# A decoder layer in split fp32 on one core: four of eight GLU chunks as seven block products, and the convolution steps handed out anew

## What is computed

```
xn = RMSNorm(x)
proj = xn @ w_in                     # B_a C_a X_a | V_b G_b | Q | three gates
ya = (a_b * dwconv3(a_c * a_x)) @ w_out_a
ub = b_val * sigmoid(b_glu)          # the GLU: G_b and V_b, 1024 columns each
yb = dwconv31(ub)                    # causal, per channel, 31 taps
yb = silu(layernorm(yb + bias)) @ w_out_b
yx = softmax(Q K^T / 16) V @ w_out_x # cross attention, 4 heads
merged = g0 * ya + g1 * yb + g2 * yx ; h = x + merged @ w_o
h = h + (silu(hn @ w_ff_gate) * (hn @ w_ff_up)) @ w_ff_down ; final RMSNorm
```

## Time and profile before

| | |
|---|---|
| median of 3 runs | 1070.38 us (1069.89 to 1071.01) |
| the profiled execution's own time | 1069.33 us |
| its span, first to last instruction | 1067.6 us |
| TensorE busy | 1057.3 us, 99% |
| VectorE busy | 718.2 us, 67% |
| ScalarE busy | 479.7 us, 45% |
| GpSimd busy | 110.8 us, 10% |
| mean granted TensorE clock | 0.997 of full |
| DMA | 187.25 MB, mean 175 GB/s |

### The profile page before, as it was taken

How to read it: one execution, slowest core, us unless ns; L and a number is a source line. 1 busy time by engine, 2 the same in 40 slices (tenths; PEclk the granted TensorE clock), 3 DMA queues, 4 the chain that set the end, 5 groups by cost and what they waited for, 6 DMA issues and landing times.

```text
span 1067.6 us, 20526 instructions
## 1 busy us (share of the span) xinstructions
PE 1057.3 (99%) x8751; PEld 1051.1 (98%) x8751; DVE 718.2 (67%) x1234; ACT 479.7 (45%) x550; POOL 110.8 (10%) x93
## 2 busy tenths in 40 slices
PE   9999999999999999999999999999999999999997
PEld 9999999999999999999999999999999999999996
DVE  6766677888888654686323755578778457588754
ACT  6744443453335353344345723344456245366431
POOL 3661000002300000000000000000000000000000
PEclk9999999999999999999999999999999999999998
DMA  8967886689796878758876663231578365487512
GB/s 293 289 189 190 222 208 154 195 228 316 215 274 140 208 172 195 177 148 192 207 187 158 160 237 116 81 99 40 152 185 198 114 148 145 119 199 176 169 41 80
DMA packets 151194, 187.25 MB, mean 175 GB/s; under 512 B 4759, under 2 KB 141295, under 8 KB 145591
## 3 DMA queue, kind: packets, MB, share of 16 engines
q1 hardware_dynamic: 117734, 106.64, 31.8%
q0 software_dynamic: 8496, 57.15, 26.7%
q10 hardware_dynamic: 24880, 22.26, 6.9%
HBM read 122.34 MB, written 7.54 MB: 122 GB/s over the span
## 4 chain that ended last, share of the span: by engine, by line
PE 96%; DVE 3%; ACT 0%; issue 0%; POOL 0%; DVEq 0%; POOLq 0%
PE acc L2218 39%; PE acc L2236 20%; PE acc L2592 12%; PE acc L2544 11%; PE acc L2551 6%; PE acc L2329 2%; PE acc L2190 2%; PE acc L2337 1%; PE acc L2433 1%; PE acc L2409 1%; DVE o_acc L1631 0%; DVE ubyb L1462 0%; DVE yA L1693 0%; PE acc L2494 0%; DVE w_l L1337 0%
## 5 line engine op out<-in xcount | busy, mean ns | idle before, releaser
L2218 PE MATMUL acc<-big_h,w_h 128*128 128x260 f32 x1664 | 337.2, 284 | 0.1
L2218 PE MATMUL acc<-big_l,w_h 128*128 128x260 f32 x1664 | 334.4, 282 | 0.0
L2218 PEld LDWEIGHTS acc<-big_h,w_h 128*128 128x128 f32 x1664 | 255.8, 188 | 0.7 <-DVE st L1667 0.3
L2218 PEld LDWEIGHTS acc<-big_l,w_h 128*128 128x128 f32 x1664 | 256.4, 189 | 0.0
L2236 PE MATMUL acc<-big_h,w_l 128*128 128x260 f32 x1664 | 209.0, 283 | 0.0
L2236 PEld LDWEIGHTS acc<-big_h,w_l 128*128 128x128 f32 x1664 | 203.7, 189 | 0.1
L1462 DVE SCALAR_TENSOR_TENSOR ubyb<-ubyb,prm 128x512 f32<-128x512 f32 (+1 forms) x240 | 180.3, 751 | 15.1 <-DVE ubyb L1462 9.4
L749 ACT ACTIVATE w_h<-w_raw 128x1024 fp32r<-128x1024 f32 x120 | 120.2, 1051 | 103.5 <-DMA w_raw<-in_w_out_a_dram 29.7
L2544 PE MATMUL acc<-x_h,ws_h 128*128 128x260 f32 x504 | 126.0, 282 | 0.0
L2544 PE MATMUL acc<-x_l,ws_h 128*128 128x260 f32 x504 | 125.8, 282 | 0.0
L2544 PEld LDWEIGHTS acc<-x_h,ws_h 128*128 128x128 f32 x504 | 94.9, 188 | 0.2
(11 more groups left out here) (278 smaller groups left out, 1327.8 us busy)
## 6 DMA issues: line engine op xcount, KB each, us to landing
w_l<-w_raw POOLq DMA_DIRECT2D x41, 1024.0 KB, 8.1
w_raw<-in_w_in_dram SPq DMA_DIRECT2D x36, 1024.0 KB, 5.3
ws_l<-w_raw POOLq DMA_DIRECT2D x18, 768.0 KB, 7.4
w_raw<-in_w_ff_gate_dram SPq DMA_DIRECT2D x18, 512.0 KB, 5.0
w_raw<-in_w_ff_up_dram SPq DMA_DIRECT2D x18, 512.0 KB, 4.9
k_st<-in_cache_mem_k_dram ACTq DMA_DIRECT2D x8, 1024.0 KB, 8.2
v_st<-in_cache_mem_v_dram ACTq DMA_DIRECT2D x8, 1024.0 KB, 12.6
w_raw<-in_w_v_dram SPq DMA_DIRECT2D x4, 1024.0 KB, 8.0
```

What stands on the lines that cost most here:

```text
L2218: last = M.matmul(out[:, b, 0:HALF], w_h[:, slot, k, cols], xs[:, k_at + k, b * HALF:(b + 1) * HALF], start=start and k == 0 and xs is x[0 ...
```

## The change

Four things are edited.

1. GLU chunks 4 to 7 (`GLU_SEVEN`) are computed by `glu_seven()`. The product of a 2 x 2 block matrix of weights and one of activations (the blocks: two 128-column halves by two halves of k, and two halves of k by two halves of the 520 rows) is done as seven block products with 12 matmuls each in place of eight. For it VectorE and ACT make sums of activation blocks once (`xn_f`, `tx_f`, `tx`), sums of weight blocks for each chunk (`glu_sums`, `glu_hi_sums`, `glu_low`), and put the results together (`glu_copy`, `glu_first`, `glu_combine`, `glu_product`). The chunk's weights are loaded as two halves of 512 KB, and POOL's adding DMA covers three of four blocks.
2. A counter `taps(count)` hands out the 256 convolution steps in order. 27 stand in the GLU stage (62 before), 32 in the query stage (34), 32 in `cx` (32), 84 in X (64), 28 in `ba` (32) and 53 in A (32: 21, 16 and 16).
3. VectorE's hardware loop in stage X is written out.
4. The `ln_sum` additions over the first seven tiles stand inside gate stage A, behind its first 21 steps. The first two `load_k` are issued in the query stage.

```diff
+GLU_SEVEN = range(4, 8)
...
+                if isinstance(c, int) and c - C_B in GLU_SEVEN:
+                    for half, b, landed_ in ((1, 0, w_half), (0, 2, w_loaded)):
+                        sp.dma_start(raw_f[:, slot, b:b + 2, :].rearrange("p a (r n) -> p (a r) n", n=P),
+                                     src[:, :, col + half * P:col + (half + 1) * P]).then_inc(landed_[slot], 16)
+                    return
...
+            split(C_B + 1, 1, T["b"] - 1)
+            for j in range(1, 8):
+                n, e = j + 1, j - 1
...
+                if n == 8:
+                    split(C_Q, 0, T["b"] + 13)
+                elif n not in GLU_SEVEN:
+                    split(C_B + n, n % 2, T["b"] + 2 * n - 3)
+                else:
+                    glu_negative(n)
+                if j in GLU_SEVEN:
+                    glu_copy(j)
+                if n in GLU_SEVEN:
+                    glu_hi_sums(n, 0)
+                    glu_hi_sums(n, 1)
+                    glu_hi_raw(n)
+                if e % 2 == 0 and e in GLU_SEVEN:
+                    act.wait_ge(acc_read, T["b"] + 2 * e + 2)
+                    nc.scalar.activation(sg[:, :, 2:SG], sg[:, :, 2:SG], ACT.Sigmoid).then_inc(b_sig, 1)
...
+            def taps(count):
+
+                nonlocal made
+                for step_ in range(made, made + count):
+                    conv(step_ // CV, [step_ % CV])
+                made += count
...
+            def glu_first(j):
+
+                u, k = T["b"] + 2 * j, nth(j)
+                m1, v, u2, _ = glu_quarters(j)
+                dve.wait_ge(b_copy, k + 1)
+                V.tensor_tensor(u2, m1, acc[u % 4][:, 1, 0:HALF], ALU.subtract).then_inc(b_uv, 1)
+                dve.wait_ge(b_uv, 2 * k + 1)
+                V.tensor_tensor(v, acc[(u + 1) % 4][:, 0, 0:HALF], u2, ALU.add).then_inc(b_uv, 1)
...
+            for j in range(1, 8):
+                n, e = j + 1, j - 1
+                if e in GLU_SEVEN:
+                    glu_combine(e)
+                    if e % 2:
+                        glu_product(e)
...
+                if n in GLU_SEVEN:
+                    glu_sums(n, 0)
+                if j in GLU_SEVEN:
+                    glu_first(j)
+                if n in GLU_SEVEN:
+                    glu_sums(n, 1)
+                    glu_low(n, 0)
+                    glu_low(n, 1)
+                taps((0, 0, 7, 6, 2, 2, 2, 6)[j])
+            glu_combine(7)
+            glu_product(7)
+            taps(2)
...
-            with dve.Fori(0, 2) as i:
-                for p in range(2):
-                    u0 = i * 8 + (T["x"] + 4 * p)
-                    conv(i + 4, Q4[2 * p])
...
+            for p in range(4):
+                u0 = T["x"] + 4 * p
+                taps(16 if p else 12)
...
+                    if j == 0:
+                        taps(6)
...
-                conv(6, range(4 * n, 4 * n + 4))
+                taps(4 if n % 2 else 3)
...
                 if it < 3:
-                    conv(KT - 1, (range(0, 11), range(11, 22), range(22, CV))[it])
+                    if it:
+                        taps((KT * CV - made) // (3 - it))
+                    else:
+                        taps((KT - 1) * CV - made)
+                        sum_first_tiles()
...
+                    for r in range(PAIRS):
+                        for m in range(2):
+                            last = M.matmul(out, weights(0, w, r), rows(m, x, r), start=r == 0 and m == 0, stop=False)
...
+                    for r in range(PAIRS):
+                        last = M.matmul(out, weights(1, w, r), rows(0, x, r), start=False, stop=r == PAIRS - 1)
```

More of the change, by code:

```diff
@@ L564, in ob, with glu_quarters @@
             return T[f"ob{n // 2}"] + n % 2
+        def glu_quarters(j):
+            if j % 2:
+                rows = ubyb[:, j:j + 2, PAD:SLOT]
+            else:
+                rows = sg[:, :, 2:SG]
+            return [rows[:, n // 2, n % 2 * HALF:(n % 2 + 1) * HALF] for n in range(4)]
         z_tmp = [ubyb[:, KT, 0:TOK], sg[:, 0, 0:TOK]]
@@ L880, in _, with turned_hi @@
             act.wait_ge(x_kept, 16 * 5)
[L883 to L893, removed]
+            def turned_hi(n):
+                act.wait_ge(t_step, 2 + n + 1)
+                nc.scalar.activation(tx[0][:, n, :, :].rearrange("p r t -> p (r t)"), tx_f[:, n, :], ACT.Copy).then_inc(t_hi, 1)
@@ new lines, in _ @@
+            split(C_B + 1, 1, T["b"] - 1)
+            for j in range(1, 8):
+                n, e = j + 1, j - 1
+                if e % 2 == 0 and e not in GLU_SEVEN:
+                    if e:
+                        act.wait_ge(acc_read, T["b"] + 2 * e)
+                    for i in range(2):
+                        done(T["b"] + 2 * e + i)
+                        nc.scalar.activation(two(sg[:, i, 2:SG]), halves(T["b"] + 2 * e + i), ACT.Sigmoid).then_inc(b_sig, 1)
+                if n == 8:
[13 more added lines that the diff above has]
+                    nc.scalar.activation(sg[:, :, 2:SG], sg[:, :, 2:SG], ACT.Sigmoid).then_inc(b_sig, 1)
+                if j == 1:
+                    for n in range(4):
+                        turned_hi(n)
@@ L921, in _ @@
                 split(C_Q + h + 1, (h + 1) % 2, T["b"] + 15 if h == 0 else T[f"q{h - 1}1"])
+                if h == 0:
+                    for u in range(2):
+                        load_k(0, u)
                 q_part(h, 0)
@@ new lines, in glu_first, with combs @@
+            def glu_first(j):
[5 more added lines that the diff above has]
+                V.tensor_tensor(v, acc[(u + 1) % 4][:, 0, 0:HALF], u2, ALU.add).then_inc(b_uv, 1)
+            def combs(j):
+                return sum(5 if n % 2 else 4 for n in range(GLU_SEVEN[0], j))
@@ L1704, in _ @@
             sample_lo(3)
-            conv(3, range(24, CV))
-            with dve.Fori(0, 2) as i:
-                for p in range(2):
-                    u0 = i * 8 + (T["x"] + 4 * p)
-                    conv(i + 4, Q4[2 * p])
[L1712 to L1719, removed]
+            taps(8)
+            for p in range(4):
+                u0 = T["x"] + 4 * p
+                taps(16 if p else 12)
+                dve.wait_ge(x_sig, 2 * p + 2)
+                for j in range(2):
+                    done(u0 + 2 + j)
+                    V.tensor_tensor(two(merged[:, 2 * p + j, :]), halves(u0 + 2 + j), two(sg[:, j, 2:SG]),
+                                    ALU.mult).then_inc(acc_read, 1 if j else 3)
+                    if j == 0:
+                        taps(6)
             def ba_lo_part(n):
```

217 lines of the change are left out of this document (180 added, 37 removed).

## The result

The changed kernel takes 1074.87 us (median of 8 runs, 1073.43 to 1076.22), the kernel before took 1070.91 beside it (8 runs). The ratio is 1.0039, with a 95% interval of 1.0028 to 1.0050: **slower by 4.0 us**. I had forecast 1072.3, with a range up to 1074.8. The profiled execution of the changed kernel took 1075.75 us with a span of 1074.0; that of before took 1069.33 with 1067.6.

What follows compares the result with a forecast made beforehand. TensorE was taken to bound the kernel. The terms -5.8 (fewer matmuls), +5.7 (wait in gate stage A) and +2.0 (clock) sum to +1.9 us, on the median of 1070.38 giving 1072.3; range 1069.8 to 1074.8.

Steps and rivals of the forecast that it cites:

- TensorE saves 5.8: GLU chunks 4 to 7: four chunks go from 11.50 to 10.05 us each, saving 5.8 us.
- Gate stage A, a wait of 5.7 (5.4 to 6.0): Third chunk of A: TensorE waits 5.7 us for VectorE's first sum, behind 21 steps and the additions.
- The clock, 2.0 (0 to 3.5): Behind stage A's stop: the clock drops to 1.2 GHz and the next chunk runs slower, costing 2.0 us.
- one to two lags: Behind stage A's stop: half speed for 2.8 to 5.6 us, which loses 1.4 to 2.8 us.
- The tightest point is chunk 4 ... It holds, by about 0.5 us. Value 0, bounds 0 and 1: GLU chunk 4: the product freeing its accumulators, behind six steps, is in time by about 0.5 us; cost 0.
- VectorE's block sums and rounding ... fall where it idles for 15 us: GLU stage's start: some 14 us of VectorE work fits its idle time or between the second and fourth chunk.
- The SP queue issues two halves for a chunk ..., 12 to 15 us ahead of need: Weight loads on the SP queue: two halves instead of one load, issued 12 to 15 us early; cost 0.
- The rival of a second stop in the GLU stage: GLU or first query chunk: a second stop costs 2 to 4 us more, 1074.3 to 1076.3; chance 0.15.
- VectorE's work of a chunk: Second-stop rival's first mechanism: 10.2 us of VectorE work a GLU chunk against 10.05 leaves its answers late.
- the query chunk's adding DMA: Second-stop rival's other mechanism, first query chunk: the DMA takes 4 us over its 8.1, eating the 1.2 us margin.
- Stage X, `ba`, `load_k`: cost 0: Branch stage X's written-out steps, `ba` with four fewer small steps, and `load_k` issued in the query stage: no cost.

Runs made afterwards that it cites:

- POOL and VectorE apart: The changed kernel, with VectorE's additions of activation blocks waiting until POOL's subtraction for GLU chunk 1 is over: 1073.50 us, ratio 1.0025.

## Why the prediction was wrong

- **TensorE saves 5.8: right.** 5.71 in the GLU stage and 6.15 in the median once no stop hides it. The sevens are fed: chunks 5 to 7 follow at 10.05 us without a wait, and the first query chunk has none either.
- **Gate stage A, a wait of 5.7 (5.4 to 6.0): right**, 5.65 between two matmul starts (5.5 without the ordinary 0.12), and the parts as well: a step each 0.79, additions 4.4.
- **The clock, 2.0 (0 to 3.5): right in mechanism, and in size as far as is known.** 1.84 in the profile of after (9.57 against 7.73), 1.7 to 2.9 in the other profiles with the full stop. By medians the stop of 5.59 costs 8.2, so 2.6 for the clock, of which some may belong to the start of the kernel. That the fall takes one to two lags was a guess that came out.
- **The step that failed** is the GLU stage's "The tightest point is chunk 4 ... It holds, by about 0.5 us. Value 0, bounds 0 and 1". The stop was 2.77 us with 1.6 of slow clock in one profile (the stage took 90.49 against 86.26 without it), 1.2 in the other, and 2.0 in all by the ratios. Two steps under it were wrong. First, "VectorE's block sums and rounding ... fall where it idles for 15 us": I asked only whether VectorE had room, not who works beside it. The additions and POOL's subtraction held each other up, 4.74 became 8.35, and through chunk 3's load and chunk 2's adding DMA this reached chunk 4's load. Second, "The SP queue issues two halves for a chunk ..., 12 to 15 us ahead of need": I took the issue for the landing. A load that is issued 4.2 us late meets the adding DMA and lands 10 us late. The count itself was sound: I had the product start 44.6 us into the GLU stage (110.31 - 66.09 + 0.4), and with the load in time (`POOL and VectorE apart`: 111.44, with the stage's start at 67.00) it starts 44.4 us into it; in the profile of after it starts 47.5 us into it. A margin of 0.5 us didn't deserve a value of 0.
- **The rival of a second stop in the GLU stage** came true in place and time (its 1074.3 to 1076.3 hold 1074.87), but not by either mechanism that I gave it: neither VectorE's work of a chunk nor the query chunk's adding DMA was late. Its chance of 0.15 was too small, since it was the only place with a margin under a microsecond.
- **Stage X, `ba`, `load_k`: cost 0, right.** No wait appears there, with six more steps in X neither. One figure was wrong without harm: before the change a pair of X had 16 steps (64 in four pairs), not 20, so 16 x 0.93 + 1.4 = 16.3 us and not 20.0; that agrees with the wait of 7.04 of a pair's 23.0.

The evidence was in the trace of before. There too one pair of POOL's subtractions takes far longer than the pair for GLU chunk 1, while VectorE works on operands in SBUF:

```profile
72.91 4.74 POOL L723 TENSOR_TENSOR w_l<-w_raw,w_h 128x1024 fp32r<-128x1024 f32 x2 [5.10 <-ACT w_h L749]
...
267.58 5.63 DVE L1631 SCALAR_TENSOR_TENSOR o_acc<-v_st,pT,o_acc 128x256 f32<-128x256 f32 x14
269.59 8.41 POOL L723 TENSOR_TENSOR w_l<-w_raw,w_h 128x1024 fp32r<-128x1024 f32 x2 [6.46 <-ACT w_h L749]
```

In sum: about -6 for the sevens, +8.2 for stage A's stop with its slow clock, +2.0 for chunk 4's; measured +4.0. These shares are steps from kernel to kernel, so that they add up proves nothing. What can be compared is the other order: with stage A already mended, the six steps at chunk 4 cost 1.4 us (1065.80 against 1064.36, with overlapping intervals), and stage A then stands for 8.7. So chunk 4's stop is worth 1.3 to 2.0 us and stage A's 8.2 to 8.7.

## What to carry to other kernels

Moving work into an engine's idle time is free only if it doesn't hold up the engine beside it, as VectorE's additions held up POOL here, or if what that engine gives back (here a buffer for a load) has slack. Where VectorE work is spread by a count, put the count behind the operation that frees accumulators, not before it: the order of six additions and six steps was worth 10 us here. Where a stop of TensorE of 2.8 us or more appeared in the middle of this kernel, the clock took 1.6 to 2.9 us more in that profile; put such a price beside the stop, and give a margin under 1 us a price of its own.

## What was not expected of the hardware

- VectorE's additions with two operands in SBUF and POOL's subtraction take turns. Alone: 2.3 for 2080 columns, 2.4 for POOL's 1024. Together: 4.52 for VectorE's second addition and 3.89 and 4.50 for POOL's two, 1.5 to 2.2 more each; VectorE's next operation, of 1040 columns, takes 3.34 beside POOL and 1.24 alone. The Trainium skill says so on the page "SBUF — State Buffer" (section "SBUF: two separate sides"): the two engines share a port pair that is an exclusive lock, and a VectorE operation with two SBUF inputs takes it against a GpSimd operation that reads SBUF. The trace agrees; had I weighed this rule, the late load would have been a rival.
- A load on SP's queue hardly moves while POOL's adding DMA runs (0.03 MB in 6 us against 1.15 MB in the 4 us after). The reverse shows as well: with a load under way from 83 to 86 us, the adding DMA issued at 82.85 moves nothing, and the load 0.76 MB.
- In the middle of the kernel the clock fell behind a stop of 2.77 us twice, both times when TensorE was at work again, and didn't behind four of 0.88 to 1.23. In the sparse work of the first ten microseconds it fell in two profiles of twelve, behind a stop of 1.63 in one and stops of 1.15 and 0.88 in the other; in two more with stops of 1.24 and 1.36 there it stayed up.
